# Second block: two gates in column tiles, one copy a place earlier on ScalarE, one dilated unit ahead of a normalization on VectorE

## The chip, the cores and the metric

The kernel runs on one core of one Trainium2 chip. The metric is the device time of one execution in microseconds, the median of three runs. Five engines work side by side and hand work on by semaphores: TensorE (PE, with its weight loads as PEld), VectorE (DVE), ScalarE (ACT), GpSimd (POOL) and SyncE (SP), which issues nearly all DMAs.

## The reference, cut to what matters

The program is a first transformer part of two layers (differential attention, a convolution, a SwiGLU) followed by a second block on 256 tokens of width 1024. In the second block the input is normalized and projected once, and the columns go to a gated delta rule (8 heads of 128, chunks of 64), to a dilated window attention (12 heads in three groups) and to two output gates. Then comes a mixture of 64 experts. What the change touches:

```
proj = h @ w_in
(gq, gk, gv, gz, gb, ga, dil_q, dil_k, dil_v, gate_a, gate_b) = split(proj)
beta = sigmoid(gb)                                   # 8 rows, one per head
g    = -exp(a_log) * softplus(ga + dt_bias)          # 8 rows, one per head
gc   = cumsum(g) in each chunk; decay = exp(gc_i - gc_j)
y_a  = _rms(o, norm_g) * silu(z)                     # of the delta rule
y_b  = sum over the groups of wts * dilated_window_attention(...)
merged = sigmoid(gate_a) * (y_a @ w_up_gdn) + sigmoid(gate_b) * (y_b @ w_up_dil)
```

## The kernel before

Each engine's program is written out by hand, in the order in which the engine runs it; nothing reorders it but a few weight loads. The second block's weights come in slots of 1 MB through a ring of six (`ORDER` names them), and `project(name)` multiplies one slot into PSUM bank 0 or 1. A slot's load is issued when TensorE is done with the slot six before it.

**The first stretch, 727 to 860 us.** TensorE runs `K0 K1`, then `decays()`, then `K2 K3 Z0 Q0 Q1 Z1 Q2 Q3 Z2 V0 ...`, with small products between them: `square_sum` (the sum of squares of a head, 2 PE instructions), `turn_kv` (4 transposes). `decays()` (L1014 to L1021) is the product of the 8 columns of `gb` and of the 8 of `ga` with the 256 tokens: for each gate 8 matmuls of 128 rows, 8 stationary columns and 256 moving ones. A float32 matmul is two PE instructions, so there are 32. Both results lie on PSUM partitions 0 to 7, beside each other in bank 4. ScalarE's `decays_first()` (L1852) reads them: L1864 the sigmoid, L1865 the other gate plus its bias.

VectorE has per projected pair a `short_conv` (L2552, six instructions), per head pair a `head_norm` (reciprocal L2491, product L2493), and between them `decays_second` and `decays_third`, which make the log decays `gdiag`. Then TensorE's `decay_rows()` (L1076) turns them into columns (L1081, bank 5) and spreads them over the partitions by four products (L1087) into banks 4, 6, 7 and last 5. The last needs bank 5 free, and so waits for ScalarE's copy of the turned gates into `tiny` (L1915, semaphore `gb_out`). ScalarE then copies the four banks into `GB` (L1917), from which GpSimd builds the decay matrices `MA` and `MB` (L2999 to L3007) and VectorE takes the last decays of the chunks (L2593). ScalarE's `conv_act(name)` (L1818 Silu, L1823 Square) waits for `short_conv(name)`, `conv_in(name)` (L1805, L1810) for the projection, `head_root` (L1765) for `square_sum`. TensorE's `square_sum("Q3")` waits for the root of Q2.

**The second stretch, 1040 to 1110 us.** TensorE projects the gates `G0` to `G7` from weights in two parts: ScalarE makes the high part (`high_of`, L1839), VectorE the low one (`low_of`, L2669). Between them run the eight units of the dilated attention, unit d by `dil_scores(d)` (PE L1034), `dil_mask(d)` (DVE L2523 to L2527), `dil_exps(d)` (ACT L1875), `dil_weights(d)` (DVE L2535 to L2541), `dil_turn(d)` (PE L1046), `dil_probs_out(d)` (ACT L1884) and `dil_out(d)` (PE L1057). `y_norm(b)` (DVE L2491, L2493, L2507) normalizes two heads of the delta rule's output and multiplies them by the silu gate. After the last, ScalarE makes `yo_hi` (L2081), VectorE `yo_lo` (L2775), and only then TensorE's first product with `y_a` (`up_gdn("UG0")`, L1320) can begin. On TensorE `dil_turn(7)` stands between `G6` and `G7`, and `dil_out(7)` behind `G7`, ahead of `UG0`.

Of the kernel before, what the change touches and what calls it, by code (L numbers as in the profile page):

```python
# [8 lines left out]
ACT = mybir.ActivationFunctionType  # L9
# [9 lines left out]
DC = D // P  # L19
# [41 lines left out]
T = SEQ  # L61
GH = 8
# [35 lines left out]
QMIX, QFFN, QADA, QC, QCW, QGN, QDQ, QDK, QAL, QDT, QRB = np.cumsum([0, 8, 8, 48, 8, 96, 1, 1, 1, 1, 1]).tolist()  # L98
# [28 lines left out]
def build(nc, args, dbg=None):  # L127
# [6 lines left out]
    with ExitStack() as ctx:  # L134
# [88 lines left out]
        ps = ctx.enter_context(nc.psum_tensor("ps", [P, 8, 512], F32))  # L223
        par2 = sb("par2", [P, NPAR2])
        w_ba = sb("w_ba", [P, DC, 16])
# [15 lines left out]
        hm = hn[:, :, 0:T]  # L241
# [359 lines left out]
        def _(pe):  # L601
            mm = nc.tensor.matmul
# [42 lines left out]
            for l in range(DEPTH):  # L645
# [152 lines left out]
                for c in range(CC):  # L798
                    m = mm(bank[:, 0:L], ones, conv[:, c, :], start=c == 0, stop=c == CC - 1)
# [7 lines left out]
                for c in range(CC):  # L807
                    m = mm(bank[:, 0:L], ones, lsq[:, c, :], start=c == 0, stop=c == CC - 1)
# [112 lines left out]
                for half in range(2):  # L921
                    for g in range(6 - 2 * half):
# [3 lines left out]
                        for n in range(4):  # L926
                            m = down(half, g, w, n)
# [6 lines left out]
                for n in range(4):  # L934
                    m = down(1, 4, w4, n)
# [4 lines left out]
                    m = down(1, 5, w5, n)  # L940
# [3 lines left out]
            for c in range(DC):  # L944
                m = mm(ps[:, 6, 0:T], ones, sq[:, c, META:L], start=c == 0, stop=c == DC - 1)
# [68 lines left out]

            def decays():

                for o in range(2):
                    for k in range(DC):
                        m = mm(ps[0:GH, 4, o * T:(o + 1) * T], w_ba[:, k, o * GH:(o + 1) * GH], hm[:, k, :],
                               start=k == 0, stop=k == DC - 1)  # L1020
                m.then_inc(ba_full, 1)  # L1021

            def dil_scores(d):
# [161 lines left out]
            for b in range(4):  # L1185
                p, heads = batch(b)
                for hh in heads:
                    m = mm(ps[:, 2 + b, (hh % 4) * P:(hh % 4 + 1) * P], MU[:, p, hh, :], gV[:, p, hh, :],
                           start=True, stop=True)
                m.then_inc(u_full, 1)  # L1190
            for b in range(4):
# [6 lines left out]
                for hh in heads:  # L1198
                    m = mm(ps[:, bank, (hh % 4) * P:(hh % 4 + 1) * P], kbg[:, p, hh, :], MU[:, p, hh, :],
                           start=True, stop=True)  # L1200
# [160 lines left out]
            for t in range(2):  # L1361
                for k in range(DC):
                    pe.wait_ge(hm_ready, DC + k + 1)
                    m = mm(ps[:, 6, t * EXPERTS:(t + 1) * EXPERTS], hm[:, k, t * P:(t + 1) * P], w_r[:, k, :],
                           start=k == 0, stop=k == DC - 1)
            m.then_inc(router_full, 1)

            for g in range(4):
                for i in range(4):
                    k = 4 * (g % 2) + i  # L1370
                    m = nc.tensor.transpose(ps[:, (4, 7, 2, 3)[g], i * P:(i + 1) * P],
                                            hm[:, k, (g // 2) * P:(g // 2 + 1) * P], ident)
# [4 lines left out]
            for b in range(2):  # L1377
                w = slot(EJ + b, ET).rearrange("p (k n c) -> p k n c", k=8, n=2)
                for n in range(2):
                    for k in range(DC):  # L1380
                        m = mm(ps[:, b, n * T:(n + 1) * T], w[:, k, n, :], hm[:, k, :], start=k == 0, stop=k == DC - 1)  # L1381
# [10 lines left out]
            for t in range(2):  # L1392
                m = nc.tensor.transpose(ps[0:EXPERTS, 6, T + t * P:T + (t + 1) * P], sel[t], ident)
            m.then_inc(ct_full, 1)
            for t in range(2):
                m = mm(ps[0:EXPERTS, 3, 0:T], sel[t], cst3[:, KR0 + t * T:KR0 + (t + 1) * T], start=t == 0, stop=t == 1)
# [110 lines left out]
            for t in range(2):  # L1507
                mm(ps[:, 3, (2 + t) * NOV:(3 + t) * NOV], combT[0:EXPERTS, t * P:(t + 1) * P], E[0:EXPERTS, :],
                   start=True, stop=True)
# [26 lines left out]
        def _(act):  # L1536
            f = nc.scalar.activation
# [275 lines left out]
            def conv_act(name):  # L1813

                n, i = CONV.index(name), int(name[1])
                act.wait_ge(gconv, n + 1)
                dst = vsg[:, i % 2] if name[0] == "V" else {"K": gk, "Q": gq}[name[0]][:, 2 * i:2 * i + 2, :]
                f(dst, gacc[:, n % 2], ACT.Silu).then_inc(gsilu, 1)  # L1818
                if name[0] != "V":
                    act.wait_ge(gsilu, n + 1)  # L1820
                    if n >= 2:
                        act.wait_ge(msum, n - 1)
                    f(sqd[:, n % 2, :], dst.rearrange("p a b -> p (a b)"), ACT.Square).then_inc(gsq, 1)  # L1823
# [29 lines left out]
            g8 = region(16512, 4, T)  # L1853

            def decays_first():
                act.wait_ge(ba_full, 1)
                CA = [0]

                def alink(ins):
                    CA[0] += 1  # L1860
                    ins.then_inc(chain_a, 1)
                    act.wait_ge(chain_a, CA[0])

                alink(f(g8[0:GH, 0, :], ps[0:GH, 4, 0:T], ACT.Sigmoid))  # L1864
                alink(f(g8[0:GH, 1, :], ps[0:GH, 4, T:2 * T], ACT.Identity, bias=par2[0:GH, QDT:QDT + 1]))  # L1865
                alink(f(g8[0:GH, 2, :], g8[0:GH, 1, :], ACT.Abs))
                alink(f(g8[0:GH, 3, :], g8[0:GH, 2, :], ACT.Exp, scale=-1.0))
                f(small[0:GH, 48:49], par2[0:GH, QAL:QAL + 1], ACT.Exp).then_inc(gate_a, 1)
# [41 lines left out]
            kv_out("K0")  # L1910
            conv_in("Q1")
            kv_out("K1")
            conv_act("Q1")
            act.wait_ge(gb_full, 1)
            f(tiny[:, 32:64], ps[:, 5, 0:32], ACT.Copy).then_inc(gb_out, 1)  # L1915
            act.wait_ge(gb_full, 2)
            f(GB[:, :, :].rearrange("p a b -> p (a b)"), flat[:, 4 * 512:8 * 512], ACT.Copy).then_inc(gb_out, 1)  # L1917
            z_out(1)
# [244 lines left out]
        def _(dve):  # L2163
# [339 lines left out]
            def y_norm(b):  # L2503
                y = yo[:, 2 * b:2 * b + 2, :]
                head_norm(f"y{b}", y, par2[:, QGN:QGN + 1])
                dve.wait_ge(mnorm, SUMS.index(f"y{b}") + 1)
                v.tensor_tensor(y, y, zs[:, 2 * b:2 * b + 2, :], ALU.mult).then_inc(ya_ready, 1)  # L2507
# [21 lines left out]
            def dil_weights(d):  # L2529

                hs, t = divmod(d, 2)
                keys = (t + 1) * P
                o, q = 16 * (d % 2), 112 + 16 * (d % 2)
                dve.wait_ge(dexp, 4 * (d + 1))
                link(v.tensor_tensor(tiny[:, q:q + 3], tiny[:, o + 4:o + 7], tiny[:, o + 8:o + 11], ALU.mult))  # L2535
                link(v.tensor_reduce(tiny[:, q + 3:q + 4], tiny[:, q:q + 3], AX_X, ALU.add))
                link(v.reciprocal(tiny[:, q + 4:q + 5], tiny[:, q + 3:q + 4]))
                link(v.tensor_scalar(tiny[:, q + 8:q + 11], tiny[:, o + 8:o + 11], tiny[:, q + 4:q + 5], None, ALU.mult))
                s_ = dS[:, d % 2, :, 0:keys]
                c_ = tiny[:, q + 8:q + 11].rearrange("p (g a) -> p g a", a=1).to_broadcast([P, 3, keys])  # L2540
                v.tensor_tensor(s_, s_, c_, ALU.mult).then_inc(dcoef, 1)  # L2541
# [18 lines left out]
            g8 = region(16512, 4, T)  # L2560
# [103 lines left out]
            def low_of(name):  # L2664

                i = PLACE[name]
                j = (B2 + i) % RING
                W(dve, "whi_ready", i - SPLIT + 1, DEPTH)
                v.tensor_tensor(wlo[j][:, :], ring[:, j, :], wb[(i - SPLIT) % 2][:, :], ALU.subtract).then_inc(wlo_ready, 1)  # L2669
# [96 lines left out]
            dil_weights(6)  # L2766
            y_norm(2)
            low_of("G6")
            y_norm(3)
            dil_mask(7)  # L2770
            low_of("G7")
            dil_weights(7)
            low_of("UG0")
            W(dve, "xhi_ready", 2, DEPTH)
            v.tensor_tensor(yo_lo[:, :, :], yo, yo_hi[:, :, :], ALU.subtract).then_inc(xlo_ready, 1)  # L2775
# [412 lines left out]
```

## Time and profile before

| | |
|---|---|
| median of three runs | 1725.96 us (1723.48 to 1726.64) |
| the profiled execution | 1725.58 us, span 1723.7 us |
| TensorE busy | 1655.5 us, 96% of the span |
| VectorE, ScalarE, GpSimd busy | 973.0, 678.2, 62.0 us |
| chain of work that ended last | PE 77%, DVE 16%, ACT 5% |

The span runs from the first to the last instruction of the core; the execution's own time is 1.9 us longer. A timeline row gives start, duration, engine, line, operation, tiles and shapes, and in brackets the idle time ahead of it and what ended it. The duration of a matmul includes a latency that overlaps the next one, so the time that an instruction costs the engine is the distance from start to start. The chain of work names at each step the engine for which the end of the program waited.

### The profile page before, as it was taken

The numbers are of one execution on the slowest core, as the hardware profiler recorded it, in microseconds if no ns is written. First come the engines' busy times: TensorE is split into PE (matmuls) and PEld (weight loads), VectorE is DVE, ScalarE is ACT, GpSimd is POOL, SyncE is SP. The second block draws the span as 40 slices with busy tenths as digits, with TensorE's granted clock in tenths as the row PEclk, the third lists the DMA queues.
The fourth block names the chain that finished last, engine by engine and source line by source line (L and its number), as shares of the span: only waits on it lengthen the run. The fifth ranks groups of instructions, "written<-read, shape, count | busy, mean of one in ns | idle before, by whom it ended". The sixth has DMA issues, their size and how long they took to land.

```text
span 1723.7 us, 27352 instructions
## 1 busy us (share of the span) xinstructions
PE 1655.5 (96%) x10886; PEld 1323.9 (77%) x10886; DVE 973.0 (56%) x1703; ACT 678.2 (39%) x1205; POOL 62.0 (4%) x48
## 2 busy tenths in 40 slices
PE   8899999998999999999999999999999999999998
PEld 6678999986789999877899998898545454545554
DVE  6977777769777777576756598765221212112121
ACT  2255434321464444364643577632223222222222
POOL 0100000001000000005120000000000000000000
PEclk9899999999999999999999999998999999999999
DMA  7222666652236667522502333446799999999995
GB/s 280 98 74 101 233 229 245 256 208 98 74 123 220 224 240 290 221 107 92 160 29 98 136 134 137 147 147 268 284 422 422 421 422 421 422 422 422 422 421 220
DMA packets 64013, 404.69 MB, mean 235 GB/s; under 512 B 12976, under 2 KB 14512, under 8 KB 15280
## 3 DMA queue, kind: packets, MB, share of 16 engines
q1 hardware_dynamic: 63488, 401.86, 59.9%
q8 instruction: 67, 1.10, 0.3%
q10 hardware_dynamic: 432, 1.51, 0.3%
q14 instruction: 26, 0.21, 0.0%
HBM read 401.91 MB, written 1.44 MB: 234 GB/s over the span
## 4 chain that ended last, share of the span: by engine, by line
PE 77%; DVE 16%; ACT 5%; issue 1%; DMA 0%; SPq 0%; DVEq 0%; ACTq 0%
PE ps L1444 21%; PE ps L846 20%; PE ps L987 10%; DVE big L2231 5%; PE ps L1435 4%; PE ps L1417 4%; PE ps L671 3%; DVE inv L2491 2%; DVE wlo L2295 2%; ACT whi L1633 2%; PE ps L1320 1%; DVE wlo L2669 1%; PE ps L1352 1%; PE ps L1381 1%; ACT wb L1839 1%
## 5 line engine op out<-in xcount | busy, mean ns | idle before, releaser
L2295 DVE TENSOR_TENSOR wlo<-ring,whi 128x2048 fp32r<-128x2048 f32 x76 | 174.2, 2292 | 90.2 <-ACT whi L1633 89.8
L846 PE MATMUL ps<-hg_hi,whi 128*128 128x272 f32 (+1 forms) x672 | 191.5, 285 | 2.4 <-DVE big L2434 2.4
L846 PE MATMUL ps<-hg_hi,wlo 128*128 128x272 f32 (+1 forms) x672 | 191.6, 285 | 0.0
L846 PE MATMUL ps<-hn_lo,whi 128*128 128x272 f32 (+1 forms) x672 | 191.0, 284 | 0.0
L1444 PE MATMUL ps<-big 128*64 128x512 f32 x816 | 181.8, 594 | 0.7 <-ACT big L2119 0.7
L1444 PE MATMUL ps<-ring,big 128*64 128x512 f32 x816 | 181.7, 594 | 0.6 <-ACT big L2136 0.6
L1633 ACT ACTIVATE whi<-ring 128x2048 fp32r<-128x2048 f32 x76 | 144.9, 1907 | 69.4 <-PE ps L846 50.9
L2955 DVE TENSOR_TENSOR ylo<-ps,yhi 128x512 fp32r<-128x512 f32 x68 | 47.0, 692 | 173.3 <-ACT yhi L2143 138.3
L1444 PEld LDWEIGHTS ps<-ring,big 128*64 128x64 f32 x816 | 57.1, 137 | 107.9 <-issue 107.5
L1444 PEld LDWEIGHTS ps<-big 128*64 128x64 f32 x816 | 57.4, 137 | 107.0 <-issue 106.6
L671 PE MATMUL ps<-hn,ring 128*128 128x272 f32 x576 | 139.2, 400 | 0.0
L2948 DVE SCALAR_TENSOR_TENSOR big<-big,ps 128x256 f32<-128x256 f32 x34 | 16.3, 481 | 205.2 <-ACT big L2132 205.2
L846 PEld LDWEIGHTS ps<-hg_hi,whi 128*128 128x128 f32 x672 | 126.6, 188 | 3.0 <-issue 2.9
L671 PEld LDWEIGHTS ps<-hn,ring 128*128 128x128 f32 x576 | 110.8, 195 | 22.5
L846 PEld LDWEIGHTS ps<-hg_hi,wlo 128*128 128x128 f32 x672 | 126.8, 189 | 0.0
L846 PEld LDWEIGHTS ps<-hn_lo,whi 128*128 128x128 f32 x672 | 126.5, 188 | 0.0
L987 PE MATMUL ps<-hn,ring 128*128 128x256 f32 x512 | 114.3, 383 | 0.6 <-ACT hn L1748 0.6
L987 PEld LDWEIGHTS ps<-hn,ring 128*128 128x128 f32 x512 | 97.7, 192 | 18.2 <-issue 5.3
L2669 DVE TENSOR_TENSOR wlo<-ring,wb 128x2048 fp32r<-128x2048 f32 x36 | 82.4, 2289 | 46.7 <-ACT wb L1839 46.5
L2231 DVE SCALAR_TENSOR_TENSOR big<-big,par 128x272 f32<-128x272 f32 x240 | 105.9, 504 | 1.5
L846 PE MATMUL ps<-hff_hi,whi 128*128 128x272 f32 (+1 forms) x352 | 101.0, 287 | 0.0
L846 PE MATMUL ps<-hff_lo,whi 128*128 128x272 f32 (+1 forms) x352 | 100.3, 285 | 0.0
(454 smaller groups left out, 3638.6 us busy)
## 6 DMA issues: line engine op xcount, KB each, us to landing
ring<-in_stream SPq DMA_DIRECT2D x277, 1024.0 KB, 5.3
big<-in_stream SPq DMA_DIRECT2D x102, 1024.0 KB, 10.7
h<-in_xT SPq DMA_DIRECT2D x1, 1088.0 KB, 5.1
out_xT<-h SPq DMA_DIRECT2D x4, 256.0 KB, 2.4
big<-in_consts ACTq DMA_DIRECT2D x1, 896.0 KB, 4.7
cst<-in_consts SPq DMA_DIRECT2D x1, 576.0 KB, 6.0
cs<-in_c_rows SPq DMA_DIRECT2D x1, 512.0 KB, 17.8
big<-in_consts ACTq DMA_DIRECT2D x1, 326.5 KB, 3.5
```

The source lines that it names most:

```text
L671: m = mm(bank[:, 0:L], w[:, k, n, :], hn[:, k, :], start=k == 0, stop=k == DC - 1)
L846: m = mm(out, a[:, at_:at_ + P], b[:, kept], start=first and i == 0, stop=last and i == 2)
L987: m = mm(ps[:, i % 2, n * T:(n + 1) * T], a, b, start=k + j == 0, stop=k == DC - 1 and j == len(pairs) - 1)
L1417: m = mm(ps[:, 1 - part % 2, (k % 2) * T:(k % 2 + 1) * T], piece[:, t, k * P:(k + 1) * P], Sf[:, t, :], start=t + i == 0, stop=t + i == 2)
L1435: m = mm(sums_of(c), piece[:, c * P:(c + 1) * P], STr[:, q, :], start=False, stop=last and i == 1, skip_group_check=True)
L1444: m = mm(out[r], lhs[:, r], ws[i], tile_position=(0, BS * i), **flags)
L1633: f(whi[d % 3][:, :], ring[:, s % RING, :], ACT.Copy).then_inc(whi_ready, 1)
L2231: m = v.scalar_tensor_tensor(conv[:, c, :], z, g, conv[:, c, :], ALU.mult, ALU.add)
L2295: v.tensor_tensor(wlo[j][:, :], ring[:, j, :], whi[d % 3][:, :], ALU.subtract).then_inc(wlo_ready, 1)
L2491: link(v.reciprocal(inv2[:, j % 2, :], root2[:, j % 2, :]))
L2669: v.tensor_tensor(wlo[j][:, :], ring[:, j, :], wb[(i - SPLIT) % 2][:, :], ALU.subtract).then_inc(wlo_ready, 1)
L2955: v.tensor_tensor(ylo[:, o], ps[:, 3 - half, :], yhi[:, o], ALU.subtract).then_inc(ylo_ready, 1)
```

## The change

Three edits, all in the second block; no instruction is added or taken away.

1. `decays()` runs over the eight weight pieces outside and over the two gates inside. Beta's 8 rows go to PSUM partitions 32 to 39 by a matmul at column tile 32, the other gate's rows to partitions 0 to 7 at column tile 0, both in the same 256 columns of bank 4. ScalarE reads them there.
2. ScalarE's copy of the turned gates stands ahead of `conv_act("Q1")`, no longer behind it.
3. On VectorE `y_norm(3)` stands behind `dil_mask(7)`, `low_of("G7")` and `dil_weights(7)`, no longer ahead of them.

```diff
             def decays():
 
-                for o in range(2):
-                    for k in range(DC):
-                        m = mm(ps[0:GH, 4, o * T:(o + 1) * T], w_ba[:, k, o * GH:(o + 1) * GH], hm[:, k, :],
-                               start=k == 0, stop=k == DC - 1)
+                for k in range(DC):
+                    for o, r in enumerate((32, 0)):
+                        m = mm(ps[r:r + GH, 4, 0:T], w_ba[:, k, o * GH:(o + 1) * GH], hm[:, k, :],
+                               start=k == 0, stop=k == DC - 1, tile_position=(0, r))
                 m.then_inc(ba_full, 1)
...
-                alink(f(g8[0:GH, 0, :], ps[0:GH, 4, 0:T], ACT.Sigmoid))
-                alink(f(g8[0:GH, 1, :], ps[0:GH, 4, T:2 * T], ACT.Identity, bias=par2[0:GH, QDT:QDT + 1]))
+                alink(f(g8[0:GH, 0, :], ps[32:32 + GH, 4, 0:T], ACT.Sigmoid))
+                alink(f(g8[0:GH, 1, :], ps[0:GH, 4, 0:T], ACT.Identity, bias=par2[0:GH, QDT:QDT + 1]))
...
             kv_out("K1")
-            conv_act("Q1")
             act.wait_ge(gb_full, 1)
             f(tiny[:, 32:64], ps[:, 5, 0:32], ACT.Copy).then_inc(gb_out, 1)
+            conv_act("Q1")
             act.wait_ge(gb_full, 2)
...
             low_of("G6")
-            y_norm(3)
             dil_mask(7)
             low_of("G7")
             dil_weights(7)
+            y_norm(3)
             low_of("UG0")
```

ScalarE, behind the turning out of the keys' second pair (L1772 is `kv_out`), - is before and + is now:

```order
 L1772 ACTIVATE big<-ps 128x2x2x128
-L1818 ACTIVATE big<-big 128x512
-L1823 ACTIVATE big<-big 128x512
-L1915 ACTIVATE tiny<-ps 128x32
+L1914 ACTIVATE tiny<-ps 128x32
+L1818 ACTIVATE big<-big 128x512
+L1823 ACTIVATE big<-big 128x512
 L1917 ACTIVATE big<-ps 128x2048
```

The small copy passed the Silu and the Square of Q1; the large copy into `GB` stands behind them as before.

VectorE before, from `low_of("G6")` (the first row) to `yo_lo`:

```order
 L2669 TENSOR_TENSOR wlo<-ring,wb 128x2048
 L2491 RECIPROCAL inv<-root 128x512
 L2493 SCALAR_TENSOR_TENSOR big<-big,par,inv 128x512
 L2507 TENSOR_TENSOR big<-big 128x512
 L2523 TENSOR_TENSOR big<-ps,big 128x768
 L2525 TENSOR_REDUCE tiny<-big 128x3
...
 L2541 TENSOR_TENSOR big<-big,tiny 128x768
 L2669 TENSOR_TENSOR wlo<-ring,wb 128x2048
 L2775 TENSOR_TENSOR yo_lo<-big,yo_hi 128x2048
```

VectorE now, the same place:

```order
 L2669 TENSOR_TENSOR wlo<-ring,wb 128x2048
 L2523 TENSOR_TENSOR big<-ps,big 128x768
 L2525 TENSOR_REDUCE tiny<-big 128x3
...
 L2541 TENSOR_TENSOR big<-big,tiny 128x768
 L2491 RECIPROCAL inv<-root 128x512
 L2493 SCALAR_TENSOR_TENSOR big<-big,par,inv 128x512
 L2507 TENSOR_TENSOR big<-big 128x512
 L2669 TENSOR_TENSOR wlo<-ring,wb 128x2048
 L2775 TENSOR_TENSOR yo_lo<-big,yo_hi 128x2048
```

The three instructions of `y_norm(3)` (L2491, L2493, L2507) moved from ahead of the unit's mask to behind its weights.

## Rows read from the trace of the kernel before

**Rows 1.** The page: busy time of the engines.
```profile
PE 1655.5 (96%) x10886; PEld 1323.9 (77%) x10886; DVE 973.0 (56%) x1703; ACT 678.2 (39%) x1205; POOL 62.0 (4%) x48
```

**Rows 2.** The chain of work, 705 to 800 us: start, us, what.
```profile
727.41 7.00 PE ps L1019 x32
...
779.42 0.09 ACT tiny L1915
...
779.56 2.07 PE ps L1087 x2
781.63 8.46 PE ps L987 x32
```

**Rows 3.** Timeline of everything, 705 to 800 us: TensorE's first three spreading products.
```profile
774.26 2.82 PE L1087 MATMUL ps<-big,cst 8*128 8x512 f32 x6
```

**Rows 4.** Stretches: us, busy PE, PEld, DVE, ACT, POOL, granted clock, DMA share, GB/s.
```profile
779.50:781.56 2.06, 2.00 (x3) 0.50 (x3) 0.00 (x0) 0.00 (x1) 0.00 (x0) 0.50 0.03 8
781.56:790.00 8.44, 8.44 (x34) 7.24 (x34) 6.38 (x4) 1.88 (x1) 6.32 (x3) 0.83 0.00 0
```

**Rows 5.** Timeline of TensorE, 115 to 117 us: products in four column tiles.
```profile
115.58 0.67 PE L718 MATMUL ps<-big 128*32 128x272 f32 x8
116.18 0.41 PE L720 MATMUL ps<-cst 128*128 128x32 f32 x2
```

**Rows 6.** The chain of work, 1235 to 1260 us: products in two column tiles.
```profile
1242.48 10.45 PE ps L1444 x48
```

**Rows 7.** Timeline of ScalarE, 705 to 826 us.
```profile
741.55 0.60 ACT L1805 ACTIVATE big<-ps 128x512 f32<-128x512 f32 x1 [3.83 <-PE ps L987]
...
781.66 1.88 ACT L1917 ACTIVATE big<-ps 128x2048 f32<-128x2048 f32 x1 [2.16 <-PE ps L1087]
...
805.97 1.91 ACT L1926 ACTIVATE big<-big 128x2048 f32<-128x2048 f32 x1
810.11 0.60 ACT L1805 ACTIVATE big<-ps 128x512 f32<-128x512 f32 x1 [2.23 <-PE ps L987]
```

**Rows 8.** Timeline of VectorE, 783 to 815 us; the second row is cut at 800.5.
```profile
783.57 6.64 DVE L2593 TENSOR_TENSOR tiny<-big,tiny 64x8 f32<-64x8 f32 x4 [5.48 <-ACT big L1917]
799.70 1.41 DVE L2552 SCALAR_TENSOR_TENSOR big<-big,par 128x256 f32<-128x256 f32 x1 [2.48 <-ACT big L1810]
799.70 3.64 DVE L2552 SCALAR_TENSOR_TENSOR big<-big,par 128x256 f32<-128x256 f32 x6 [2.48 <-ACT big L1810]
811.47 2.71 DVE L2552 SCALAR_TENSOR_TENSOR big<-big,par 128x256 f32<-128x256 f32 x6 [4.15 <-ACT big L1810]
```

**Rows 9.** Timeline of GpSimd: the last two products of the decay matrices.
```profile
796.63 4.20 POOL L3007 TENSOR_TENSOR big<-big,tiny 128x1024 f32<-128x1024 f32 x2
```

**Rows 10.** Timeline of TensorE, 816 to 826 us: the square sum of Q3.
```profile
824.80 1.10 PE L1005 MATMUL ps<-big,cst 128*128 128x512 f32 x2
```

**Rows 11.** Timeline of TensorE, 1089 to 1111 us.
```profile
1089.27 1.46 PE L1034 MATMUL ps<-big 128*128 128x256 f32 x6
...
1100.65 0.87 PE L1046 MATMUL ps<-cst,big 128*128 128x128 f32 x6 [3.60 <-DVE big L2541]
...
1109.82 0.36 PE L1320 MATMUL ps<-yo_hi,wb 128*128 128x256 f32 x1
```

**Rows 12.** Timeline of VectorE, 1089 to 1107 us.
```profile
1089.57 3.35 DVE L2491 RECIPROCAL inv<-root 128x512 f32<-128x512 f32 x1
...
1094.35 0.95 DVE L2523 TENSOR_TENSOR big<-ps,big 128x768 f32<-128x768 f32 x1
...
1096.60 2.28 DVE L2669 TENSOR_TENSOR wlo<-ring,wb 128x2048 fp32r<-128x2048 f32 x1
...
1104.61 2.28 DVE L2775 TENSOR_TENSOR yo_lo<-big,yo_hi 128x2048 fp32r<-128x2048 f32 x1
```

**Rows 13.** Timeline of ScalarE, 1100 to 1105 us.
```profile
1102.26 1.90 ACT L2081 ACTIVATE yo_hi<-big 128x2048 fp32r<-128x2048 f32 x1
1104.06 0.80 ACT L1884 ACTIVATE big<-ps 128x768 f32<-128x768 f32 x1
```

## The prediction, made before the changed kernel ran

> **What bounds the kernel now.** I read the page first: TensorE is busy 96% of the span [rows 1], so a gain has to take work or a wait out of TensorE's own line. Then the chain of work: the 32 instructions of the gates' product (L1019, 7.00 us) lie on it, and so do the turned gates' copy, the spreading product behind it and the Z1 projection [rows 2]. Then the timelines of each engine around the three places. All times below are in the clock of the kernel before, "now" is what I work out for the changed one.
>
> **Edit 1, the gates in two column tiles.** Before, 32 instructions of 256 columns take 7.00 us, 0.219 each [rows 2]. Column tiles occur elsewhere in this kernel. The experts' products, in two tiles in turns, take 10.45 us for 48 instructions of 512 columns [rows 6]: 0.218 each for twice the columns, so two tiles run at once and a column costs half. At that rate the gates need 32 x 0.109 = 3.5 us. Products of 272 columns in four tiles, 8 of them, hold the engine for 116.18 - 115.58 = 0.60 us [rows 5]; a quarter of 8 x 0.219 x 272/256 would be 0.465, so going in and out of the tiles costs some 0.14. I take 3.65, a saving of 3.35. The bounds are 0 (no overlap) and 3.5. Is it on the path? K2's projection follows at once; ScalarE waited 3.83 us for it before its copy at 741.55 [rows 7], and it is done with the gates before that even now. VectorE waits for that copy, and then runs without a gap to the end of Q1's convolution. So all of this moves by 3.35.
>
> The tile page puts a price against the edit: the Trainium skill, TensorEngine Tiling (Array Packing), Key Properties, says that changing the tiling mode, though not the tile, drains TensorE. The 0.14 us above is what the trace shows of it; without it the saving would be 3.5 and the sum 1714.3; if every change of tile drained, it would be the last rival below.
>
> **Edit 2, the copy one activation sooner.** Three of the four spreading products run 774.26 to 776.85 (six instructions, 0.43 each) [rows 3]. The fourth starts at 779.56, when the copy, which stood behind Q1's Silu and Square, has ended at 779.5 [rows 2]. What it copies is there from 774.4 on, and ScalarE is free at 775.0. So the copy is done by 775.2, ahead of need, and the stall of 779.56 - 776.85 = 2.7 us goes. It delays Q1's Silu by nothing: that waits for VectorE until 778.1. The stall has a second price: after it the granted clock is 0.50, then 0.83 [rows 4], that is 1.2 GHz and then back to 2.4. The fourth product takes 2.07 us where two such instructions take 0.86 at full clock, and Z1 takes 8.46 [rows 2] where the other projections take 6.91. Without the stall TensorE has no gap here, so 1.2 + 1.55 us come back. TensorE ends Z1 earlier by 3.35 + 2.7 + 1.2 + 1.55 = 8.8 us, at 781.3 for 790.1.
>
> **What is late next.** ScalarE's copy into GB stands behind Q1's Silu and Square, so it moves from 781.66 [rows 7] only to 779.4 less 3.35, about 776.0: by 5.6. GpSimd's building of the matrices and VectorE's last decays follow it. There is a collision in the rows: VectorE's four tiny subtractions take 6.64 us, and the first product of Q2's convolution 1.41 where six take 2.71 undisturbed; it ends when a GpSimd product ends [rows 8, 9]. So a two-input VectorE instruction waits out the GpSimd one that is running. GpSimd's eight products now last from 778.1 to some 796, while Q2's convolution can start at 799.70 - 8.8 = 790.9: two or three collisions for one. By hand: its first step waits for a product until 791.6 and ends at 792.05, the second is held until 793.95, the third until 796.3, then four at 0.45: it ends at 798.1, where a shift of 8.8 alone gives 794.5.
>
> Most of that lag is covered. VectorE had 4.15 us to spare ahead of Q3's convolution [rows 8], but ScalarE only 2.23 ahead of its copy of Q3 [rows 7]: behind Q2's convolution stand Silu, Square, a table load and the exponential of MA, from 803.3 to 807.9 [rows 7]. Now they end at 798.1 + 4.5 = 802.6, so the copy of Q3 moves by 810.1 - 802.6 = 7.5. From there ScalarE is packed up to the root of Q2, and TensorE's square sum of Q3 waits for that root: it starts at 824.80, at the moment the root is there [rows 10], so there is no slack. TensorE then stands about 1.3 us. Shorter gaps than 1.3 us elsewhere are followed by full speed, so I add no clock loss. From there on every engine is 7.5 us earlier, and the weight loads with them, since each waits for a slot that TensorE frees. **Stretch one gives 7.5 us**, 8.8 if there is no collision.
>
> The rule behind the collision is in the Trainium skill, SBUF — State Buffer, SBUF: two separate sides: an exclusive lock between VectorE with two SBUF inputs and GpSimd, held for a whole instruction. The 1.41 and 6.64 us rows agree. By a reading without it the sum is that of the second rival.
>
> **Edit 3, the last unit first.** The scores of unit 7 run at 1089.27 for 1.46 us [rows 11], so they are ready at 1090.7; VectorE is free for them at 1089.6 and instead normalizes until 1094.4 [rows 12]. Now the mask starts at 1090.75 and not at 1094.35 [rows 12]: 3.6 earlier. Its four steps end at 1093.0, G7's low part follows (its high part was ready at 1091.9), ScalarE's exponentials run beside it, and the weights end at 1097.0. TensorE ends G6 at 1096.9 and before stood 3.60 us until 1100.65 [rows 11]; now 0.15. G7 runs to 1103.4.
>
> The moved normalization now takes 1096.9 to 1101.8 (its steps end 4.85 after its start [rows 12]). yo_hi starts at 1101.8 for 1102.26 and ends at 1103.7, and the probabilities' copy ends at 1104.4 [rows 13]: TensorE waits for it 1.1 us ahead of the last unit's product (1.3 us, to 1105.7). VectorE makes UG0's low part until 1104.0 and yo_lo until 1106.2 (2.28 [rows 12]). So UG0 starts at 1106.2 and not at 1109.82 [rows 11]. **Stretch two gives 3.6 us**; between ends of 0.0 and 3.6, since even with the mask as late as before yo_lo would be ready at about 1109.9. From UG0 on the chain is TensorE's with waits that move along, and the experts' loads wait for TensorE too, so I carry the 11.1 to the end.
>
> **Sum.** Against the profiled execution's own 1725.58: less 7.5 and 3.6 is **1714.5**. That execution is 0.4 from the median 1725.96, which I leave out.
>
> **The rivals.**
> - *No overlap of the tiles.* Eight stationary columns may leave something else as the limit. For it: no row here has so few. Against it: [rows 5, 6]. The 3.3 us are missing: 1717.8.
> - *No collision worth counting.* GpSimd and VectorE fall otherwise than by my hand count; the first stretch gives 8.8: 1713.2.
> - *GB's copy sets the pace.* If the matrices, not the projections, end last behind 777, the whole stretch moves by 5.6 as that copy does: 1716.4. Against it: VectorE and ScalarE have waits on TensorE there [rows 7, 8].
> - *Slower: every change of tile drains the array.* Place: the 32 instructions of the gates. Run one by one each would cost its load and its full duration, 0.09 + 0.38 = 0.47 us in this trace, so 15.0 for 7.00; that eats 8.0 and, with 3.35 not gained, leaves 1725.8. The gaps would also take the clock to half, as in [rows 4]: 30 us, so about 1741. It decides for slower from 0.46 us an instruction. Against it: 0.218 and 0.075 an instruction in [rows 5, 6].
> - *The change doesn't do what it says*: the second or third edit's stall is only handed on to another wait, and 8 or more of the 11.1 are lost: within 0.2%.
>
> **How the numbers follow.** Forecast 0.60; no overlap 0.09; no collision 0.13; GB's copy 0.10; handed on 0.05; drain 0.03. Run times before spread by 3 us, which I add in half on each side: 1713.2 less 1.5 and 1717.8 with 1.0 make the range 1711.7 to 1718.8; it leaves out the last two and a little. About 0.2% (3.4 us) is what a measurement of this kernel can tell from no change. Faster 0.92, same 0.05, slower 0.03.
>
> **What would show it.** L1019's 32 instructions in 3.5 to 3.8 us for 7.00. The copy L1914 at 771 to 772, L1087 eight in a row without a wait, the granted clock 1.00 there, Z1 in 6.91 us. A wait of about 1.3 us of TensorE for the square sum of Q3, with Q2's convolution at 5 to 7 us for 3.64. L1046's last wait under 0.3 for 3.60, one of 1.1 ahead of L1057 and one of 0.5 ahead of L1320. I am wrong if L1019 takes 7 us, if another wait over 2 us stands between 778 and 860, or if the step from UG0 to the end, 613.9 us, grows.

## The result, and the profile of the changed kernel

The changed kernel takes 1713.86 us (median of four runs, 1713.32 to 1715.80) against 1725.51 us for the kernel before in the same comparison. The ratio is 0.9936, with a 95% interval of 0.9919 to 0.9953: faster by 0.64%. The prediction was 1714.5, in a range of 1711.7 to 1718.8. The profiled execution took 1713.32 us, with a span of 1711.5 for 1723.7.

The timeline of TensorE of the changed kernel, 711 to 817 us (start, duration, engine, line, operation, tiles, shapes, count, and in brackets the wait ahead of it):

```profile
711.70 14.05 PE L987 MATMUL ps<-hn,ring 128*128 128x256 f32 x64 [0.61 <-ACT hn L1748]
725.68 3.63 PE L1019 MATMUL ps<-hn,w_ba 128*8 128x256 f32 x32
...
769.16 3.78 PE L1087 MATMUL ps<-big,cst 8*128 8x512 f32 x8
...
816.31 1.10 PE L1005 MATMUL ps<-big,cst 128*128 128x512 f32 x2
```

The 32 products of the gates take 3.63 us for the 7.00 of [rows 2]. All eight spreading instructions (L1087) now stand in a row, where [rows 3] showed six and then a stall. But the Z1 projection behind them is no faster. The chain of work of the same kernel (start, duration, engine, tile, line, count) has it at 8.64 us for 8.46 [rows 2]:

```profile
769.30 3.64 PE ps L1087 x8
772.94 8.64 PE ps L987 x32
```

Stretch by stretch (busy time of each engine, the granted clock, the DMA share, GB/s), the changed kernel behind 771 us:

```profile
771.00:772.90 1.90, 1.90 (x6) 0.55 (x4) 1.83 (x5) 0.00 (x0) 0.00 (x0) 0.92 0.60 246
772.90:775.00 2.10, 2.10 (x6) 1.74 (x6) 0.09 (x1) 1.95 (x3) 0.00 (x0) 0.50 0.00 0
775.00:777.00 2.00, 2.00 (x8) 1.63 (x8) 0.87 (x2) 1.08 (x1) 0.78 (x1) 0.74 0.00 0
```

TensorE is busy for the whole of each stretch, and yet the clock falls to 0.50, which is 1.2 GHz, and comes back to 2.4 GHz as it did in [rows 4]. The stall is gone; the low clock behind it is not.

The collision of VectorE with GpSimd is there (VectorE's timeline), and ScalarE (its timeline) shows what it costs:

```profile
787.64 2.11 DVE L2493 SCALAR_TENSOR_TENSOR big<-big,inv 128x512 f32<-128x512 f32 x1
791.19 4.46 DVE L2552 SCALAR_TENSOR_TENSOR big<-big,par 128x256 f32<-128x256 f32 x6 [1.44 <-ACT big L1810]
```

```profile
801.60 0.60 ACT L1805 ACTIVATE big<-ps 128x512 f32<-128x512 f32 x1 [1.39 <-PE ps L987]
```

The scaling takes 2.11 us and Q2's convolution 4.46, which took 3.64 in [rows 8]. ScalarE still waits 1.39 us for TensorE ahead of its copy of Q3 (2.23 in [rows 7]), so the collision uses up some of ScalarE's slack and costs no time.

The second stretch, TensorE and then VectorE:

```profile
1088.61 0.87 PE L1046 MATMUL ps<-cst,big 128*128 128x128 f32 x6
1096.12 1.58 PE L1057 MATMUL ps<-big 128*128 128x128 f32 x12 [0.96 <-ACT big L1884]
1097.83 0.35 PE L1320 MATMUL ps<-yo_hi,wb 128*128 128x256 f32 x1
```

```profile
1082.30 0.96 DVE L2523 TENSOR_TENSOR big<-ps,big 128x768 f32<-128x768 f32 x1 [1.11 <-PE ps L1034]
...
1095.45 2.28 DVE L2775 TENSOR_TENSOR yo_lo<-big,yo_hi 128x2048 fp32r<-128x2048 f32 x1
```

The 3.60 us wait of [rows 11] is gone. A wait of 0.96 stands ahead of L1057, and UG0 begins when `yo_lo` ends.

To compare profiles I cut each by four starts on TensorE: K0 (L987, ahead of the gates), L1161 (the first product of the delta rule's inverse), L1034 (the scores of unit 7) and L1320 (UG0). In us:

| kernel | K0 starts | K0 to L1161 | L1161 to L1034 | L1034 to UG0 | UG0 to the end |
|---|---|---|---|---|---|
| before | 713.36 | 148.38 | 227.53 | 20.55 | 613.88 |
| changed | 711.70 | 141.55 | 227.55 | 17.03 | 613.67 |
| difference | 1.66 | 6.83 | 0.0 | 3.52 | 0.21 |

The sum is the 12.2 us of the spans. The 1.66 ahead of K0, where no code differs, is no effect of the change; it goes with a different granted clock there. The granted clock in the first part, kernel before and then the changed one:

```profile
480.00:485.00 5.00, 3.33 (x22) 2.95 (x22) 3.25 (x5) 3.22 (x10) 0.00 (x0) 0.90 0.00 0
485.00:490.00 5.00, 4.40 (x24) 3.79 (x23) 2.03 (x9) 3.83 (x6) 0.00 (x0) 0.76 0.00 0
```

```profile
480.00:485.00 5.00, 3.03 (x23) 2.45 (x21) 2.54 (x3) 3.57 (x13) 0.00 (x0) 1.00 0.00 0
485.00:490.00 5.00, 3.18 (x20) 2.57 (x21) 3.27 (x13) 2.20 (x3) 0.00 (x0) 1.00 0.00 0
```

Some executions lose the clock there and some do not (and likewise at 60 to 80 us, where the mean is 0.74 before and 0.83 for the changed kernel); in the fourteen profiles K0 started anywhere from 710.93 to 713.95. So the change itself is worth 6.83 + 3.52 = 10.35 us in the traces. The medians differ by 11.65; medians of four runs each, with spreads of 3.2 and 2.5 us, do not tell these apart.

### The profile page after: what moved, and what is told of

It reads as the page before. It is cut to its first block, busy times and chain, and to the rows that moved or that the text cites. A ratio compares the mean times of both kernels' runs of the same rounds, so it can differ in the third digit from the quotient of the medians.

```text
span 1711.5 us, 27352 instructions
## 1 busy us (share of the span) xinstructions
PE 1647.1 (96%) x10886; PEld 1318.2 (77%) x10886; DVE 974.7 (57%) x1703; ACT 679.8 (40%) x1205; POOL 62.2 (4%) x48
## 4 chain that ended last, share of the span: by engine, by line
PE 78%; DVE 15%; ACT 4%; issue 1%; DMA 0%; SPq 0%; DVEq 0%; ACTq 0%
PE ps L1444 21%; PE ps L846 20%; PE ps L987 11%; DVE big L2231 5%; PE ps L1435 4%; PE ps L1417 4%; PE ps L671 3%; DVE wlo L2295 2%; ACT whi L1633 2%; DVE inv L2491 2%; PE ps L1320 1%; PE ps L1352 1%; DVE wlo L2669 1%; PE ps L1381 1%; PE ps L708 1%
## 5 line engine op out<-in xcount | busy, mean ns | idle before, releaser
L987 PE MATMUL ps<-hn,ring 128*128 128x256 f32 x512 | 114.5, 383 | 0.6 <-ACT hn L1748 0.6
L987 PEld LDWEIGHTS ps<-hn,ring 128*128 128x128 f32 x512 | 97.7, 192 | 17.7 <-issue 4.7
```

Of the source, the lines that this page charges most:

```text
L987: m = mm(ps[:, i % 2, n * T:(n + 1) * T], a, b, start=k + j == 0, stop=k == DC - 1 and j == len(pairs) - 1)
```

## Experiments: each edit alone

The theory is three separate savings that add up; the rival, that one of them needs another, or is handed on to a later wait.

**The tiles alone (e1_tiles)**, the kernel before with the edit below (its matmul line shortened) and ScalarE's two reads as in the change:

```diff
-                for o in range(2):
-                    for k in range(DC):
-                        m = mm(ps[0:GH, 4, o * T:(o + 1) * T], w_ba[...], hm[:, k, :],
-                               start=k == 0, stop=k == DC - 1)
+                for k in range(DC):
+                    for o, r in enumerate((32, 0)):
+                        m = mm(ps[r:r + GH, 4, 0:T], w_ba[...], hm[:, k, :],
+                               start=k == 0, stop=k == DC - 1, tile_position=(0, r))
```

> The kernel before with the first edit alone, the gates in two column tiles. Theory: the 32 instructions of the gates' product take 3.6 us for 7.00, everything behind moves by 3.4, the turned gates' copy still holds the fourth spreading product back by 2.7 us and Z1 takes 8.5 us. Ratio to before 0.998. Rival (the gain is swallowed by ScalarE's work on the gates or by a later wait): the stretch from the start of K0's projection to the start of L1161, 148.38 us before, stays within 1 us.

Measured: 1720.79 us (1720.04 to 1722.31), ratio 0.9978 (0.9968 to 0.9988) against 1725.18 before. K0 to L1161 takes 145.01, 3.37 less. The stall stays:

```profile
775.24 2.07 PE L1087 MATMUL ps<-big,cst 8*128 8x512 f32 x2 [2.47 <-ACT tiny L1915]
777.25 8.61 PE L987 MATMUL ps<-hn,ring 128*128 128x256 f32 x32
```

**The copy alone (e2_copy)**, the kernel before with ScalarE's copy one place earlier

```diff
-            conv_act("Q1")
             act.wait_ge(gb_full, 1)
             f(tiny[:, 32:64], ps[:, 5, 0:32], ACT.Copy).then_inc(gb_out, 1)
+            conv_act("Q1")
```

> The kernel before with the second edit alone, the copy ahead of Q1's Silu. Theory from the changed kernel's trace: the stall of 2.7 us goes, the eight spreading instructions take 3.6 us in a row, but the clock falls all the same and Z1 stays at 8.4 to 8.8 us. K0's start to L1161's start falls by 3.4 us, ratio 0.998. Rival (what I had predicted): the clock fell through the stall alone, so here Z1 takes 6.9 us and the stretch falls by 4.2 to 5.4 us.

Measured: 1720.82 us (1719.23 to 1723.22), ratio 0.9977 (0.9968 to 0.9986). K0 to L1161 takes 145.02, 3.36 less. The eight spreading instructions run without a wait (timeline), and the clock falls behind them all the same (stretch):

```profile
773.39 3.67 PE L1087 MATMUL ps<-big,cst 8*128 8x512 f32 x8
```

```profile
777.00:779.00 2.00, 2.00 (x6) 1.65 (x6) 0.21 (x1) 1.72 (x3) 0.00 (x0) 0.50 0.02 4
```

From the start of L1087 to that of Z1 it is 3.60 us for the 7.30 of before, so 3.70 less; Z1 itself takes 0.3 more. So the low clock at Z1, which I had put down to the stall, comes without it.

**The unit alone (e3_unit)**, the kernel before with

```diff
-            y_norm(3)
             dil_mask(7)
             low_of("G7")
             dil_weights(7)
+            y_norm(3)
```

> The kernel before with the third edit alone, unit 7 ahead of the last normalization. Theory: UG0's first product starts 3.6 us earlier counted from unit 7's scores, 20.55 us before and 16.9 here; nothing earlier changes; ratio 0.998. Rival (the wait is handed on to yo_lo): 20 us or more. Together with the first two, the three parts add up to the whole, 3.4 + 3.4 + 3.6 = 10.4 us, if none hides another.

Measured: 1721.48 us (1720.04 to 1725.93), ratio 0.9983 (0.9974 to 0.9992). K0 to L1161 takes 148.50, as before; L1034 to UG0 17.03 for 20.55. The three gains of 0.22, 0.23 and 0.17% (each with an interval of 0.1% either way) add up to 0.62% for the 0.64 of the whole, and in the traces 3.37 + 3.36 us add up to 6.73 for the 6.83 of the first stretch, with 3.52 for 3.52 in the second: the edits don't need each other.

The run with the copy alone shows what the 3.52 consists of. There too TensorE waits for unit 7, but this time the clock stays up behind the wait (its timeline, then a stretch that begins 1.6 us behind the wait's end). The last fence is a stretch of the kernel before, 1.4 us behind the end of the wait of [rows 11], at 0.50:

```profile
1096.37 0.88 PE L1046 MATMUL ps<-cst,big 128*128 128x128 f32 x6 [3.57 <-DVE big L2541]
```

```profile
1098.00:1100.00 2.00, 2.00 (x19) 2.00 (x18) 1.89 (x1) 2.00 (x3) 0.00 (x0) 1.00 0.03 8
```

```profile
1102.00:1104.00 2.00, 2.00 (x11) 2.00 (x10) 1.60 (x1) 2.00 (x2) 0.00 (x0) 0.50 0.03 8
```

L1034 to UG0 then takes 19.01. So about 2.0 us of edit 3 are waiting saved (3.6, less 1.6 of new waits behind G7, counted from start to start), and 1.5 are a low clock behind the wait. Three of the four traces looked at with this wait have it (the kernel before, e1_tiles, e5_before_rows128); e2_copy's execution, the fastest of its eleven at 1719.23, has not, and one trace doesn't tell chance from an effect of the copy.

## Experiments: what brings the clock down at Z1

**Products of 128 rows instead of 8 (e4_rows128).** The spreading product multiplies 8 rows of `gdiag` with ones. Theory: not the stall but these products bring the clock down, because TensorE multiplies with only 8 of its 128 rows in them, though the profile calls it busy. The changed kernel with

```diff
-                    m = mm(ps[:, 4 + b, :], ones[0:GH, :], gdiag[0:GH, 2 * b:2 * b + 2, :], start=True, stop=True)
+                    m = mm(ps[:, 4 + b, :], ones, gdiag[:, 2 * b:2 * b + 2, :], start=True, stop=True)
```

and with `gdiag` set to zero once by GpSimd, long before.

> The changed kernel with the four spreading products over 128 rows in place of 8: rows 8 to 127 of the right-hand side are set to zero beforehand by GpSimd, which is idle then, so the result and the number and size of the instructions on TensorE are the same. Theory (the granted clock falls because products of 8 rows leave the array nearly idle): the clock stays at 1.00, L1087's eight instructions take 3.45 us and Z1 takes 6.9 us for 8.6. TensorE then ends Z1 1.9 us sooner, and the collision that I predicted (VectorE's convolution of Q2 held by GpSimd) decides how much arrives: L1161 0.6 us (collision lag in full) to 1.9 us (none) sooner. Rival (the gap of 0.4 us, the transposes or something else brings the clock down): Z1 stays at 8.6 us and the time is that of the changed kernel.

Measured: 1715.22 us (1713.29 to 1715.46), ratio 0.9938 (0.9925 to 0.9952). The products cost the same, and Z1 comes back to full speed (timeline and one stretch). The wait of 0.4 us and the four transposes of 8 rows (L1081) just ahead of them are there as before, so these don't bring the clock down by themselves:

```profile
770.53 3.70 PE L1088 MATMUL ps<-big,cst 128*128 128x512 f32 x8
774.07 7.07 PE L988 MATMUL ps<-hn,ring 128*128 128x256 f32 x32
```

```profile
773.00:775.00 2.00, 2.00 (x8) 1.20 (x7) 1.25 (x3) 0.64 (x2) 0.00 (x0) 1.00 0.24 86
```

K0 to L1162 (its L1161) takes 139.80, 1.75 less than in the changed kernel. But the time is not less. The 1.5 us went here, behind two short waits at 850 us (timeline, then a stretch):

```profile
850.83 0.63 PE L1012 MATMUL ps<-cst,big 128*128 128x128 f32 x4 [1.38 <-ACT big L1786]
852.79 3.56 PE L1162 MATMUL ps<-big 128*128 128x128 f32 x16 [1.32 <-ACT big L1786]
```

```profile
852.00:854.00 2.00, 1.21 (x6) 1.24 (x7) 0.00 (x0) 0.64 (x3) 0.00 (x0) 0.65 0.64 270
```

The changed kernel has the same two waits and takes 2.02 us for these 16 instructions.

**The stall without the 8-row products (e5_before_rows128)**: the kernel before, with the same edit.

> The kernel before, with one thing changed: the four spreading products take 128 stationary rows instead of 8 (the other 120 rows of the moving operand are zeros, set once by GpSimd), so the same sums come out. The 2.5 us wait of TensorE ahead of the fourth product stays. Question: what brings the granted clock down there, the products of 8 rows or the wait. Theory A (the rows do it, the wait does nothing): all eight instructions at 0.43 us each, the fourth product 0.9 us instead of 2.07, Z1 6.9 to 7.1 us instead of 8.46, so about 2.7 us less than before, 1722.5. Theory B (the wait alone is enough): Z1 stays at 8.3 to 8.7 us, the granted clock shows 0.5 right behind the wait, the time is that of before, 1725.2. I give A 0.6: in this kernel other waits of 1.3 to 3.6 us were followed by full clock in some executions and by half clock in others.

Measured: 1725.11 us (1723.66 to 1726.63), ratio 0.9997 (0.9988 to 1.0007). Theory A is right on Z1 and wrong on the time (it said 1722.5):

```profile
779.35 1.13 PE L1088 MATMUL ps<-big,cst 128*128 128x512 f32 x2 [2.38 <-ACT tiny L1916]
780.32 7.07 PE L988 MATMUL ps<-hn,ring 128*128 128x256 f32 x32
```

A wait of 2.38 us, and Z1 at full clock behind it: here the stall did not bring the clock down, the 8-row products did. K0 to L1161 takes 145.89, 2.49 less than before. Then 1.6 are given back at L1161 (its first 16 instructions take 3.27, and from L1161 to L1034 it is 229.1 for 227.5) and 1.1 behind unit 7's wait (L1034 to UG0: 21.66 for 20.55). 2.5 less 2.7 leaves nothing, as measured.

**Is the loss at 850 tied to the 128 rows?** The changed kernel and e4_rows128 once more:

> The changed kernel once more, for times on the same chip as the three others. By its first four runs 1713.9 us. Z1 takes 8.6 us, the first 16 of L1161 2.02, the stretch from K0 to L1161 141.55. What of its length differs from profile to profile lies upstream of K0 (its start was at 711.70 in the first profile, at 711.65 to 713.95 in others with the same code ahead of it) and behind UG0 (613.0 to 614.4).

> The changed kernel with spreading products of 128 rows once more, for a second profile and for times on the same chip as the others. If the lowered clock behind the waits at 850 belongs to this kernel, the first 16 of L1161 take 3.3 to 3.6 us again; if it was chance, 2.02. The time stands within 0.5 us of the changed kernel: the 1.75 us of Z1 are given back there, 1713.8 to 1715.3.

Measured, on one chip: 1713.39 us (1712.59 to 1715.43) and 1714.91 us (1712.87 to 1715.06). K0 to L1161 was 141.56 and 139.81; the first 16 of L1161 took 2.02 and 3.44. Over all profiles with the waits at 850: with 8 rows (low clock at Z1) eight of eight had 2.02, with 128 rows (full clock at Z1) four of four had 3.27 to 3.56. So a low clock of about the same price comes at the next waits when the one at Z1 is gone. Why the waits at 850 bring it in the one case and not in the other, these runs don't show.

**Filling the two waits (e9_rows128_fill, e10_fill).** If that low clock needs the waits, it has to go when they are filled. In e9_rows128_fill, products that nobody reads run in them:

```diff
             turn_kv("V2")
+            pe.wait_ge(mroot, SUMS.index("Q3") + 1)
+            for _ in range(9):
+                mm(ps[:, 2, 0:P], ones, ident, start=True, stop=True)
             turn_kv("V3")
+            for _ in range(9):
+                mm(ps[:, 2, 0:P], ones, ident, start=True, stop=True)
```

> The changed kernel with spreading products of 128 rows, and with nine products of 128 columns more (into a bank that nobody reads then) ahead of each of the two waits of 1.38 and 1.32 us that TensorE has at about 850. All three runs with 128 rows had a low granted clock right behind these waits (the first 16 of L1161 in 3.27 to 3.56 us), all seven with 8 rows had it not (2.02). Theory (the lowered clock was not taken away with the 128 rows but moved on to the next waits, and these need TensorE idle): each wait shrinks to 0.3 to 0.5 us, the first 16 of L1161 take 2.0, the stretch from K0 to L1161 stays at 139.8, and the time falls by 1.5 us against 128 rows alone, to 1712.2 to 1713.7, below the changed kernel. Rival (it comes whatever the waits, or elsewhere later): L1161 stays at 3.3 to 3.5 us or another stretch takes it up, and the time stays at that of 128 rows alone.

> The changed kernel with its spreading products of 8 rows, with the same eighteen products of filling at 850: the control for the run before. There is no low clock behind these waits in the changed kernel, so both theories say: L1161 in 2.02, the stretch at 141.5, the time that of the changed kernel within 0.5 us. If the filling itself costs something (ScalarE is not held by it, TensorE by at most what exceeds the wait), it shows here.

Measured: **1711.39 us** (1710.77 to 1713.24) with 128 rows, ratio 0.9923 (0.9910 to 0.9937); 1714.91 us (1714.44 to 1715.70) with 8 rows. The timeline of e9_rows128_fill at 850, and a stretch of it:

```profile
849.43 2.17 PE L1148 MATMUL ps<-cst 128*128 128x128 f32 x18
...
851.88 2.17 PE L1151 MATMUL ps<-cst 128*128 128x128 f32 x18
853.88 1.95 PE L1167 MATMUL ps<-big 128*128 128x128 f32 x16
```

```profile
853.00:857.00 4.00, 4.00 (x38) 4.00 (x37) 0.00 (x0) 1.42 (x3) 1.98 (x2) 1.00 0.09 37
```

With the waits gone the clock stays at 1.00, and the 16 instructions take 1.95. The median lies below the 1712.2 to 1713.7 that I had expected, and the waits don't shrink to 0.3 to 0.5, they vanish: a float32 product is two instructions, so each filling takes 2.0 us and not 1.0, more than the wait it fills. That costs 0.96 of the stretch (K0 to L1161 140.76 for 139.80 or 139.81; in the control 142.50 for 141.55, 0.95 of the 1.5 us by which the control lies above the changed kernel, where I had expected at most 0.5). K0 to the next projection, dq0, takes 166.86, against 167.44 and 167.34 with 128 rows alone and 167.72 in the changed kernel. So up to dq0 it gains 0.9 us on the changed kernel. Its median is 2.0 us below that kernel's on the same chip, but the two ranges overlap (up to 1713.24, and from 1712.59), so a gain beyond the 0.9 is not shown. Less filling, no longer than the wait it fills, would give up to 0.96 more, an estimate from what the filling costs here; no run shows it.

## Experiments: the tiles in turns, and the collision

**One tile after the other (e6_one_by_one)**, the changed kernel with

```diff
-                for k in range(DC):
-                    for o, r in enumerate((32, 0)):
+                for o, r in enumerate((32, 0)):
+                    for k in range(DC):
```

> The changed kernel, with the gates' 32 products in the same two column tiles, but all 16 of the first tile and then all 16 of the second, not in turns. Theory (two tiles overlap only where neighbours in the row lie in different tiles): the 32 instructions take 6.9 to 7.2 us instead of 3.63, and the time is 3.4 above the changed kernel, 1717.3. Rival (a product of 8 columns is short by itself, whatever its neighbour): they stay at 3.6 to 3.9 us and the time at 1713.9.

Measured: 1716.25 us (1715.24 to 1716.67), K0 to L1161 144.18, 2.63 longer than in the changed kernel:

```profile
725.63 6.22 PE L1019 MATMUL ps<-hn,w_ba 128*8 128x256 f32 x32
```

So 2.6 of the 3.44 us come from the two tiles taking turns. Both expectations missed: the instructions take 6.22, not 6.9 and not 3.6, which is 0.19 each for 0.219 outside of tiles. Why one tile after the other is a little quicker than no tiles stays open.

**ScalarE's copy into GB sooner (e8_gb, and e7_rows128_gb with 128 rows too)**: `conv_act("Q1")` behind that copy.

> The changed kernel with one thing moved: ScalarE's copy into GB ahead of Q1's Silu and Square. Theory (the collision of VectorE with GpSimd is covered, so relieving it brings nothing): Q2's convolution takes 3.6 us instead of 4.46 and its first scaling 1.1 instead of 2.1, ScalarE's wait ahead of its copy of Q3 grows from 1.4 to 2.0 or more, the first stretch stays at 141.5 and the time within 0.5 us of the changed kernel, 1713.9. Rival (my prediction's collision: TensorE waits for it at the square sum of Q3): the stretch falls by about 1 us and so does the time.

Measured: 1715.85 us (1714.65 to 1718.69). K0 to L1161 141.53. ScalarE's timeline has its wait back at the length of [rows 7], and Q2's convolution, at 3.63, is back at that of [rows 8]:

```profile
803.39 0.60 ACT L1805 ACTIVATE big<-ps 128x512 f32<-128x512 f32 x1 [2.23 <-PE ps L987]
```

The collision is back to what it was before the change, and the stretch stays, so it was not the bound. The time missed my 1713.9 by 2 us. The profiled execution, 2.5 us above that of the changed kernel, has 1.8 of this ahead of K0 (713.49) and 0.75 behind UG0 (614.42), where it runs the changed kernel's code.

> The changed kernel with spreading products of 128 rows (as in the run before it of that kind) and with ScalarE's copy into GB ahead of Q1's Silu and Square instead of behind them. The run with 128 rows alone had the first stretch, from the start of the K0 projection to the first L1161, at 139.8 us for 141.55, and VectorE's Q2 convolution at 5.87 us, held three times by GpSimd's instructions. Theory (the collision is now the limit, its cover just used up): GpSimd starts its eight products 3 to 3.5 us sooner, Q2's convolution takes 3.6 to 4.5 us, but TensorE has nothing earlier to do with that, so the stretch stays at 139.7 to 140.0 and the time within 1 us of the run with 128 rows alone: 1713 to 1715. Rival (ScalarE is late for TensorE behind Q2): the stretch falls by up to 1 us, to 138.8. A second question: whether the 1.5 us of lower clock behind the two short waits at 850, seen there once, comes again (then L1161 takes 3.5 us for its first 16 instructions, otherwise 2.0).

Measured: 1715.29 us (1713.18 to 1716.43). K0 to L1162 139.79, the first 16 of L1162 in 3.44. Q2's convolution took 4.93, where I had expected 3.6 to 4.5, for 5.87 with 128 rows alone: counted from K0, GpSimd starts only 1.2 us sooner (63.23 for 64.47) and not 3 to 3.5, and so the two still meet; ScalarE's wait ahead of Q3 came to 0.94 instead of none. The stretch did not move.

## Why the prediction was right, step by step

- **Edit 1**: forecast 3.65 for the 32 instructions and so 3.35 saved; from their start to that of the next projection it is 3.56, which saves 3.4. Two tiles in turns run at once, as [rows 6] said of the experts' products. The Trainium skill, TensorEngine Tiling (Array Packing), Key Properties, says also that different tiles can load and multiply in parallel. The runs agree: 3.63 us with the tiles in turns, 6.22 with one tile after the other.
- **Edit 2, the stall**: forecast 2.7 + 1.2 = 3.9 up to the start of Z1; measured 7.30 - 3.71 = 3.59, from the start of L1087 to that of Z1.
- **Edit 2, the clock behind it: the step that failed.** "Without the stall TensorE has no gap here, so 1.2 + 1.55 us come back." The 1.2 came, within the 3.59. The 1.55 at Z1 did not: 8.64 for 8.46, so -0.2. I had taken the low clock for an effect of the stall because it came behind it. Ahead of the low clock stood a second thing, the spreading instructions of 8 rows; the four cases show that it is they: with 8 rows Z1 is slow with the stall (8.54 us by the timeline) and without it (8.71), with 128 rows it is fast with the stall (7.07, e5) and without it (7.07, e4). The trace of the kernel before had a hint that I overlooked: the granted clock is 0.76 from 777 to 778 us and 0.50 from 778 to 779, so it fell in the first microsecond of the stall, which lasted 2.7. With 128 rows the 1.55 do come back at Z1, and 1.5 are lost at 850.
- **The collision**: right in kind (2.11 and 4.46 us), wrong in its price of 1.3. I had the convolution end at 798.1 less the start of K0, 84.7; it ended at 795.65, only 83.95 behind K0, although Z1 ended 1.9 us later than assumed. That left ScalarE 1.39 us of slack. With Z1 at full speed the convolution takes 5.87 and ScalarE's wait is gone, but still no engine is late: K0 to L1161 shortens by 8.58, close to the 8.8 of the rival without a collision.
- **Stretch one**: forecast 7.5, measured 6.83. Up to the end of Z1 I had 8.8 and the traces have 6.85: 1.7 less by the clock at Z1, 0.3 less by the stall, 0.1 more by the tiles. Against these 1.9 stand the 1.3 of the collision that were not lost. The two errors cancel in large part, so the 7.5 was close partly by luck.
- **Edit 3**: forecast 3.6, measured 3.52, with a wait of 0.96 for 1.1 ahead of L1057 and UG0 bound to `yo_lo`. What I had not seen is that UG0 was not bound to `yo_lo` before (it ended at 1106.89 by [rows 12], UG0 began at 1109.82) but to TensorE's own line, slowed behind the wait, so that 1.5 of the 3.52 hang on a low clock that the trace of e2_copy doesn't have.
- **The rivals**: no overlap and a drain at every change of tile are ruled out by the 3.63 us for 32 instructions. GB's copy does not set the pace: moved ahead, it changes the stretch by 0.02. Handed on to another wait: the stalls were not; the clock's share of edit 2 never came in the changed kernel, and where it did come, with 128 rows, it was lost again at 850.
- **The median**: 10.35 in the traces against 11.65 between medians; 1725.58 less 10.35 is 1715.2, inside the range. The 1.3 us by which the median is lower lie within the scatter of the runs.

## What to carry to other kernels

A low granted clock behind a stall is not proof that the stall made it: look at what TensorE ran just ahead, and ask of products with few rows whether it was they. When a low clock is taken away in one place, another can come at the next short gap, so a saving of clock is counted at the end of the chain, not where it shows. Compare profiles by stretches between fixed instructions; whole spans of this kernel differ by 3 us with no change of code.

## What the runs showed of the hardware

- Eight float32 instructions with 8 rows and 512 columns, 3.6 us in all without a gap, bring the granted clock from 1.00 to 0.50; with 128 rows, at the same 3.7 us, it stays at 1.00. The Trainium skill, TensorE: Matmul & The Clock Gate, Part 1: The HAM clock gate, says that the clock follows how busy the array has been. The profile's busy row can't show whether this case agrees: it reads 1.90 of 1.90 us from 771 to 772.9, where the clock began to fall, and is as full in e4_rows128 (2.00 of 2.00 from 771 to 773), where the clock stayed at 1.00.
- A wait of 2.38 us left the clock at 1.00, one of 3.57 likewise (e2_copy), one of 3.60 was followed by 0.50 in the kernel before, and two of 1.38 and 1.32 by 0.65 and then 0.50 with 128 rows, by 1.00 with 8. So the length of a wait alone does not decide; what does, these runs don't explain.
- The scaling on VectorE with two operands from SBUF took 0.69 us alone and 1.05 to 2.58 beside GpSimd's products. The Trainium skill, SBUF — State Buffer, SBUF: two separate sides, says that the one waits for the other's whole instruction. These rows agree: in the changed kernel the scaling of 2.11 us ended at 789.75, 0.6 us behind the change from one GpSimd product to the next at 789.15, and in e7_rows128_gb the one of 2.58 us ended at 790.72, 0.6 behind such a change at 790.13.
